# Eight row buffers instead of five for the first modulation, and the first ScalarE table loaded ahead of its data

## What is computed

```
c_act = jax.nn.silu(c)                                   # c: 1 x 1024
mod = c_act @ ada_w[layer] + ada_b[layer]                # ada_w[0]: 1024 x 6144
sh1, sc1, g1, sh2, sc2, g2 = split(mod, 6)
hmix = rmsnorm(x, norm_mix[layer]) * (1.0 + sc1) + sh1   # x: 512 x 1024
proj = hmix @ hg_w_in                                    # 1024 x 4096
```

## Time and profile before

| | |
|---|---|
| time, median of 3 runs | 2317.79 us (2316.93 to 2318.14) |
| the profiled execution | 2317.2 us, its span 2315.9 us |
| TensorE busy | 2272.5 us, 98% of the span |
| VectorE busy | 1631.4 us, 70% |
| ScalarE busy | 1050.0 us, 45% |
| GpSimd busy | 667.8 us, 29% |
| transfers | 304.44 MB, mean 131 GB/s |

### The profile page before, as it was taken

One profiled execution on the slowest core, in us unless ns is written; L12 is line 12 of the kernel. 1 busy time (PEld: TensorE's weight loads), 2 busy tenths in 40 slices (PEclk: granted clock), 3 DMA queues, 4 the chain that ended last, 5 costly groups with the idle time before them and its releaser, 6 DMA issues.

```text
span 2315.9 us, 33916 instructions
## 1 busy us (share of the span) xinstructions
PE 2272.5 (98%) x13715; PEld 1978.5 (85%) x13715; DVE 1631.4 (70%) x2087; ACT 1050.0 (45%) x1515; POOL 667.8 (29%) x587
## 2 busy tenths in 40 slices
PE   7999999999999999999999999999999999999999
PEld 5888977999887877777999888999888778899987
DVE  6655857988885446736988656988555984788844
ACT  4322244555434348834555445444345363544442
POOL 0111522333122038813333011333010871233200
PEclk9999999999999999999999999999999999999999
DMA  8665024776673310015775535775233212777422
GB/s 294 189 200 164 1 91 134 189 187 155 211 248 103 100 58 1 2 57 145 190 180 130 164 96 159 176 180 146 91 100 93 82 37 73 189 178 178 111 91 82
DMA packets 224082, 304.44 MB, mean 131 GB/s; under 512 B 14313, under 2 KB 165414, under 8 KB 223926
## 3 DMA queue, kind: packets, MB, share of 16 engines
q1 hardware_dynamic: 172980, 219.79, 29.5%
q0 software_dynamic: 50640, 82.29, 17.4%
q10 hardware_dynamic: 306, 0.19, 0.0%
HBM read 300.13 MB, written 2.10 MB: 131 GB/s over the span
## 4 chain that ended last, share of the span: by engine, by line
PE 84%; DVE 9%; POOL 3%; issue 2%; ACT 2%; DMA 1%; ACTq 0%; DVEq 0%; POOLq 0%
PE ps L724 46%; PE ps L1135 10%; PE ps L1137 10%; PE ps L1136 10%; DVE w_lo L2246 2%; DVE dsa_mask L2972 1%; POOL hg_k L3272 1%; PE ps L1261 1%; POOL nsa_p L3362 1%; PE ps L1277 1%; DVE small L2970 1%; DMA m_raw<-in_ada_w 1%; PE ps L696 1%; DVE h_lo L2343 1%; DVE feat_t L2619 0%
## 5 line engine op out<-in xcount | busy, mean ns | idle before, releaser
L2246 DVE TENSOR_TENSOR w_lo<-w_raw,w_hi 128x1024 fp32r<-128x1024 f32 (+1 forms) x466 | 650.5, 1397 | 501.8 <-ACT w_hi L1589 500.7
L1589 ACT ACTIVATE w_hi<-w_raw 128x1024 fp32r<-128x1024 f32 (+1 forms) x472 | 495.8, 1051 | 988.2 <-PE ps L724 645.0
L1135 PE MATMUL ps<-feat_t,w_hi 128*128 128x256 f32 x1152 | 326.5, 283 | 3.1 <-DVE hid L2668 2.3
L1136 PE MATMUL ps<-feat_t,w_hi 128*128 128x256 f32 x1152 | 326.0, 283 | 0.0
L1137 PE MATMUL ps<-feat_t,w_lo 128*128 128x256 f32 x1152 | 326.0, 283 | 0.0
L3196 POOL TENSOR_TENSOR w_raw<-w_raw,w_raw 128x1024 f32<-128x1024 f32 x72 | 178.7, 2482 | 457.5 <-DVE w_lo L2246 457.5
L724 PE MATMUL ps<-h_hi,w_hi 128*128 128x512 f32 (+1 forms) x776 | 306.3, 395 | 3.7 <-DVE w_lo L2246 2.1
L724 PE MATMUL ps<-h_hi,w_lo 128*128 128x512 f32 (+1 forms) x776 | 302.2, 389 | 0.0
L724 PE MATMUL ps<-h_lo,w_hi 128*128 128x512 f32 (+1 forms) x776 | 302.1, 389 | 0.0
L1135 PE MATMUL ps<-h_hi,w_hi 128*128 128x256 f32 x864 | 244.9, 283 | 1.9 <-DVE w_lo L2246 1.9
L1136 PE MATMUL ps<-h_lo,w_hi 128*128 128x256 f32 x864 | 244.5, 283 | 0.0
(11 more groups left out here) (438 smaller groups left out, 4191.5 us busy)
## 6 DMA issues: line engine op xcount, KB each, us to landing
w_raw<-in_ffn_w_up SPq DMA_DIRECT2D x126, 512.0 KB, 6.3
w_raw<-in_ffn_w_down SPq DMA_DIRECT2D x176, 256.0 KB, 3.4
w_raw<-in_ffn_w_up POOLq DMA_DIRECT2D x72, 512.0 KB, 7.5
m_raw<-in_ada_w POOLq DMA_DIRECT2D x56, 512.0 KB, 4.7
w_raw<-in_ffn_w_gate SPq DMA_DIRECT2D x54, 512.0 KB, 6.0
w_raw<-in_hg_w_in SPq DMA_DIRECT2D x64, 256.0 KB, 3.2
w_raw<-in_ffn_w_up SPq DMA_DIRECT2D x48, 256.0 KB, 3.1
w_raw<-in_nsa_w_in SPq DMA_DIRECT2D x40, 256.0 KB, 2.9
```

What stands on the lines that cost most here:

```text
L1135: K.nc.tensor.matmul(out, hi[:, w], m_hi, start=opens and kt == f == 0, stop=False, skip_group_check=True)
L1136: K.nc.tensor.matmul(out, hi[:, w], m_lo, start=False, stop=False, skip_group_check=True)
L1589: K.nc.scalar.activation(K.half(K.hi(u), width), K.half(K.raw(u), width), ACT.Copy) \
L2246: K.nc.vector.tensor_tensor(K.half(K.lo(u), width), K.half(K.raw(u), width), hi, ALU.subtract) \
```

## The change

`FIRST` goes from 5 to 8. The three new buffers are the slots 1, 2 and 3 of the ring of raw weights, which are free until weight loads 1 to 3. Their landings are counted on the semaphores of those slots. In `weights(n)`, SP waits before loads 1, 2 and 3 until DVE has finished the last unit that used the slot: units 13, 14 and 15. ACT gets an activation of a constant with the function Silu ahead of its wait for the turned vector tile.

```
-FIRST = 5
+FIRST = 8
...
-        self.first_landed = [sem(f"first_landed{i}") for i in range(FIRST)]
+        self.first_landed = [sem(f"first_landed{i}") for i in range(FIRST - 3)] + self.raw_landed[1:RAW]
...
-        self.first = [self.m_raw[0][:, :], self.m_raw[1][:, :]] + [self.m_acc[:, k, :] for k in (2, 3, 4)]
+        self.first = [self.m_raw[0][:, :], self.m_raw[1][:, :]] + [self.m_acc[:, k, :] for k in (2, 3, 4)] + [self.w_raw[k][:, :] for k in (1, 2, 3)]
...
     def weights(n):
         key, slot, pieces = K.loads[n]
+        if 1 <= n < RAW:
+            sp.wait_ge(*K["mod_ready"].at(("first", max(u for u in range(2 * KD) if u % FIRST == n + 4))))
         raw_free(K, sp, key, K.raw_before[n])
...
-            .then_inc(*K.first_landed[u % FIRST].up(u, 16))
+            .then_inc(*K.first_landed[u % FIRST].up(("first", u), 16))
...
     act.wait_ge(*K["small_vec"].at("eps"))
+    nc.scalar.activation(K.small[:, 1:2], K.eps, ACT.Silu)
     act.wait_ge(*K["vec_copied"].at(0))
     nc.scalar.activation(K.cvec[:, :], K.v["c"], ACT.Silu).then_inc(*K["small_act"].up("c"))
...
-        dve.wait_ge(*K.first_landed[slot].at(u))
+        dve.wait_ge(*K.first_landed[slot].at(("first", u)))
```

## The result

| | before | after |
|---|---|---|
| median of 20 runs each | 2317.20 us (2316.41 to 2319.80) | 2321.59 us (2320.48 to 2322.51) |
| ratio | | 1.0016, 95% interval 1.0010 to 1.0022 |
| span of the profiled execution | 2315.9 us | 2319.6 us |
| TensorE busy | 2272.5 us | 2273.8 us |

The change makes the kernel 4.4 us slower by the medians and 0.16% by the ratio, which is 3.7 us. The interval leaves no doubt about the sign. The prediction had 2318.5 us and a range up to 2320.9: it missed by 3.1 us, and the time lies outside the range.

A forecast was written before the change was run, and what follows sets the result against it. TensorE's matmuls bound the kernel (98% busy), so the change could only shift their start at 40.26 us. -0.3 + 1.3 = +1.0 us on 2317.2 gave 2318.2; half of 0.6 added, 2318.5 us, range 2315.3 to 2320.9.

The forecast's parts named there:

- The table load: Start: moving the 1.28 us load ahead makes silu(c) ready near 9.2 us; gain 0 on the path, bound 0.2 us.
- Three units ahead of the small transfers: Transfer queue at the start: units 5 to 7 delay the small vectors by 3.9 us, to 21.1 instead of 17.18.
- VectorE: After unit 12 (29.03) it waits for part 0's sum at 30.7; units 13 to 15 end at 34.95 against 34.55.
- The bound of 0.65 us: VectorE step: weight loads 1 to 3 no longer mix with units 13 to 15; gain at most half a weight load.
- The fill sets the second sum: Before part 1's sum: TensorE's fill ends at 35.96, later than VectorE's 34.95, so the fill sets that sum.
- The clock in the norm: Sums of squares: 6.2 us of TensorE idleness lowers the clock; +1.3 us taken, between 0 and 1.6.
- the 8 to 9.5 that the prediction named as its sign: Norm: TensorE's sums of squares taking 8 to 9.5 us was one sign that the prediction was right.
- TensorE's end of the start: Last fill and first products: full clock without idle time ends the fill at 40.2 and returns 0.24 us; -0.3 us.
- Weight loads 1 to 3: Issued after units 13 to 15, load 1 there by 36 us, ACT wants it at 39.17 or later; cost 0.
- The slower rival: TensorE stays at half clock through squares, sums and fill: 9 to 13 us more, 2326 to 2330 us; chance 0.04.
- The forecast of +1.0: Sum for the whole start: -0.3 + 1.3 = +1.0 us on the profiled execution's 2317.2, giving 2318.2.

The follow-up runs named there:

- small transfers moved, nothing else: Kernel before (five buffers) with only the eleven small vector transfers moved behind unit 7: 2321.14 us, ratio 1.0016.
- changed, TensorE kept busy: Changed kernel with 13 more filling matmuls between the transposes of x and the wait for the small vectors: 2319.20 us, ratio to before 1.0006.
- changed, 7 fills: Changed kernel with 7 instead of 12 filling matmuls behind the first sum: 2320.59 us, ratio to before 1.0009.
- small on ScalarE, load 0 last: Changed kernel with small transfers issued from ScalarE's queue, 13 filling matmuls behind the first sum, weight load 0 behind unit 15: 2316.68 us, ratio to before 0.9991.
- without the five fills: Kernel before without the five filling matmuls ahead of the first products: 2318.19 us, ratio 1.0004.
- with the small transfers on ScalarE's queue: Changed kernel with the eleven small transfers issued from ScalarE's queue and 17 filling matmuls behind the first sum: 2316.30 us, ratio to before 0.9992.
- with 13 fills: Changed kernel with small transfers issued from ScalarE's queue and 13 filling matmuls behind the first sum: 2317.39 us, ratio to before 0.9998.
- VectorE's four operations moved: Lower-bound operations moved behind weight unit 2's low part: in the changed kernel 2320.72 us; with small transfers on ScalarE, 13 fills, load 0 behind unit 15, 2316.39 us.
- the last of the runs above: Changed kernel, small transfers on ScalarE's queue, 13 fills, load 0 behind unit 15, VectorE's four lower-bound operations behind weight unit 2's low part: 2316.39 us, ratio 0.9993.

## Why the prediction missed

| | second sum starts | late by | marker late by |
|---|---|---|---|
| before | 34.61 | | |
| changed | 38.26 | 3.65 | 3.6 |
| small transfers moved, nothing else | 38.47 | 3.86 | 3.8 |
| changed, TensorE kept busy | 35.73 | 1.12 | 1.1 |
| changed, small transfers back | 34.06 | -0.55 | -0.6 |
| changed, 7 fills | 37.91 | 3.30 | 3.3 |
| before, early table | 35.01 | 0.40 | 0.4 |
| small on ScalarE, load 0 last | 32.34 | -2.27 | -2.2 |

Each row is one profiled execution. The second sum's lateness arrives at 1767 us in all of these, and to 0.1 us also in the runs without the five fills (-1.07 and -1.0), with the small transfers on ScalarE's queue (-0.81 and -0.9) and with 13 fills (-1.02 and -1.0). The two executions where it does not are those with VectorE's four operations moved, told above. The steps in the prediction's own order:

- *The table load*, gain 0: right, 0.12 us at VectorE's first unit.
- *Three units ahead of the small transfers*, 3.9 us: right, 3.83.
- *VectorE* waiting for the sum of part 0: right in kind. What I called 1.8 us of waiting was 4.99, with the clock's part in it and unit 12 finished sooner. The bound of 0.65 us on how much sooner units 13 to 15 could land was too low. Unit 15 landed at 31.3 (10.2 us after its issue at 21.1) instead of 33.25.
- *The fill sets the second sum*: right. The sum started 0.9 us behind VectorE's last unit (38.26 against 37.32) where 1.0 was forecast, and the run with less fill gave 0.8 of it back.
- *The clock in the norm*, +1.3 us between ends of 0 and 1.6: undersized. It cost 2.36, by the squares in the two profiles and by the run that kept TensorE busy. The price was that of a low stretch of 3.5 us. Here the low level lasted from 19.7 to 26.6 us, and 5.6 us of that met work, nearly all of it the sums of squares. They took 9.99 us, outside the 8 to 9.5 that the prediction named as its sign.
- *TensorE's end of the start*, -0.3 us: the step that failed. I credited 1.4 us for the last fill at full clock (3.84 to 2.40) and 0.24 for the first products, and checked only the first tile of `hmix` behind them. All of that credit happened: the last fill ended only 2.1 us late (42.37 against 40.26), and unit 1 started 2.3 us late (48.15 against 45.83). But unit 2 started 3.6 us late, at 54.83 against 51.27, after an idle time of 0.95 us for its low part. These are that low part and TensorE's first product with it in the kernel before, and then the low part in the kernel after:

```profile
49.91 1.22 DVE L2246 TENSOR_TENSOR w_lo<-w_raw,w_hi 128x1024 fp32r<-128x1024 f32 x1
51.27 0.47 PE L724 MATMUL ps<-h_hi,w_hi 128*128 128x512 f32 x1
```

```profile
53.46 1.22 DVE L2249 TENSOR_TENSOR w_lo<-w_raw,w_hi 128x1024 fp32r<-128x1024 f32 x1
```

  The product follows the end of the low part by 0.14 us before (51.13 to 51.27) and by 0.15 after (54.68 to 54.83). So there was no room on this path even before, where the texts of the runs above speak of 0.3 us: TensorE and VectorE reached unit 2 together, and a gain on TensorE alone had nowhere to go. The trace of the kernel before held this chain, and I did not follow it past its first link.
- *Weight loads 1 to 3*, cost 0: right. Load 1 was issued at 34.6 and landed by 38.9; ScalarE wanted it at 42.7.

- *The slower rival*: its price was not added up right. If a third of the squares' 7.63 us is waiting, half speed costs 5.1 + 5.4 = 10.5 us and not 9. It did not come about: the clock was back at 1.00 by 26.6 us, and the first fill took its 5.43 us.

Put together: by the prediction's own steps the second sum was to start at 35.96 + 1.3 = 37.26 us, 2.65 late. The forecast of +1.0 took 1.65 off for the credit. Without that, and with 1.06 more for the clock (2.36 instead of 1.3), it is 3.7 us, the difference of the spans. The other 0.4 us of the miss is that the median of the runs stands 0.66 above the profiled execution (2321.59 against 2320.93), where 0.3 had been added. So the mechanism up to the second sum was foreseen, with the clock's part too small. The size and the range were wrong mainly because they held a gain that the path could not take.

## What to carry to other kernels

Where buffers are added to a ring, look at what else stands in the same queue behind them, however small; here eleven transfers of 0.1 MB in all, put behind three more units of 512 KB, cost 4 us, as an engine waited for them in program order. A gain on one engine must be followed through every link behind it until the slack is known, not just to the first consumer. And where an idle stretch grows, the work behind it is to be costed at the lower clock too; here 5.6 us of work at half clock cost 2.4 us.

## What the runs showed that was not expected

- The fall of the clock moves from execution to execution. In the run without the five fills the wait for the small vectors was 2.37 us, as in the kernel before, and still the clock was at 0.50 from 17 to 20 us and the squares took 8.95 us. In the earlier trace rows the same wait had cost nothing, and neither had longer ones in two other executions: 2.81 us with the early table alone and 3.19 us with the small transfers back, both with squares of 7.64 us.
- There is a second such place at about 1795 us, ahead of the sparse attention's scores. In the run with TensorE kept busy the marker at 1767 us was 1.1 us late, but the span 2.8 us longer than before, and TensorE's clock at 1790 to 1810 us read 0.91 and 0.92, where it reads 1.00 in the kernel before with the same 2.0 us of idleness in the first of the two stretches:

```profile
1790.00:1800.00 10.00, 7.98 (x36) 6.01 (x35) 9.24 (x18) 6.31 (x10) 2.58 (x2) 0.91 0.31 84
1800.00:1810.00 10.00, 10.00 (x42) 8.19 (x41) 7.45 (x12) 1.80 (x4) 4.14 (x1) 0.92 0.24 76
```

  Four of the profiled executions have it (also that without the five fills, the one with VectorE's operations moved in the changed kernel, and the one with weight load 0 last), and between the marker and the end they lose 1.6 to 1.7 us. That blurs gains of this size in the medians. It may be a part of the scatter of 3 us in the runs, which is not shown.
- Narrow sums pay for the low clock too: 16 records of one column took 2.75 us where the clock fell to 0.50 some 0.9 us after their start (the last of the runs above), and 1.84 to 1.97 at full clock.
- Open: in three of the runs unit 15 landed only at 32.2 to 32.7 us, though the transfer engines moved only 115 to 260 GB/s from 30 to 33 us there. In the changed kernel it was there at 31.3. Weight load 1 was issued at about 30 us in those runs; whether it held back the last shares of unit 15 was not tried.
